# Two transformer blocks on one core: the matmuls' moving tiles are placed at the same byte modulo 512 as the weight tiles

## The chip, the cores and the metric

The kernel runs on one core of a Trainium2 chip. The metric is the device time of one execution, in microseconds (us); lower is better. Engines are called PE (TensorE, the matrix engine, with its weight loads listed apart as PEld), DVE (VectorE), ACT (ScalarE), POOL (GpSimd) and SP (SyncE, which issues most of the transfers).

## The reference

Two blocks work on a sequence of 512 positions with 1,024 channels, all in float32. The first block normalises its input, projects it, runs four heads of gated linear attention and eight heads of softmax attention with low-rank queries and keys, and multiplies the joined heads by an output matrix; a multilayer perceptron (MLP) of width 4,096 and a gated per-layer input follow. The second block has two layers: a windowed mean mixer and then a banded chunk attention of 16 heads, each followed by a gated feed-forward network (FFN) of width 2,816 with a causal convolution of three taps. Cut to what the change touches:

```
h = h + concat([o_g, o_m]) @ w_out                      # attention output parts
m = rms_norm(h); h = h + square(relu(m @ w_up)) @ w_down    # MLP, 1024 -> 4096 -> 1024
gate = sigmoid(rms_norm(h) @ w_ple_gate + b)
h = h + (p @ w_ple_proj) * gate                         # per-layer input p
x = x + pool_mixer(h) ; x = x + chunk_attention(h) @ w_o
x = x + (silu(conv3(h @ w_gate)) * (h @ w_val)) @ w_ffn_out   # FFN, 1024 -> 2816 -> 1024, twice
```

## The kernel before

**Number format.** Every large product is made of three fp32r matmuls. Each operand is split into a high part (its fp32r rounding) and a low part (the rest): weights into WH and WL, the normed input into AH and AL, the activations of the MLP and FFNs into HH and HL, the heads' outputs into OM and LM (softmax heads of the first block), OH and OL (second block) and the per-layer input into pH and pL. The helper `triple` (lines 583 to 587) issues high x high, high weight x low input, low weight x high input:

```
e.matmul(o, a, h, start=first, stop=False)      # L585: stationary WH, moving AH / HH / OM / OH / pH
e.matmul(o, a, l, start=False, stop=False)      # L586: stationary WH, moving AL / HL / LM / OL / pL
return e.matmul(o, c, h, start=False, stop=last)  # L587: stationary WL, moving AH / HH / OM / OH / pH
```

In `triple` the weights (128 columns of 4 bytes, so 512 bytes of each partition) are the stationary operand, which a weight load brings in ahead of each matmul, and the activations (512 columns, 2,048 bytes) are the moving one. `triple_t` (L591 to L593) turns the roles round: activations stationary, weights moving. It serves the value and query products and, in the mixer of the second block (`mix_rows`), HH and HL as stationary operands with 256 moving columns of the weights. A row of the profile names both operands, moving and stationary, in no fixed order of role: `bank<-HH,WH` at L585 is moving HH, stationary WH; `bank<-WH,HH` at L591 is moving WH, stationary HH.

**Order of the work.** Weights come in 136 units of up to 1 MB through two raw buffers (RAW), are rounded by ACT into one of three WH buffers (L1287) and subtracted by DVE into one of three WL buffers (L1677). PE goes through a written order (`mlp_order`, `ffn_order`, `attend_order`): for the MLP four groups of eight "up" tiles (moving AH, AL) each followed by eight "down" tiles (moving HH, HL, 8 chunks each); for each FFN three groups of 8, 8 and 6 gate and value tiles (AH, AL) and eight output tiles (HH, HL). One such run of "down" or output tiles is 8 tiles x 8 chunks x 3 = 192 matmuls, or 144 in the last group of an FFN; over the kernel that makes 8 runs of 192 and 2 of 144, 1,824 matmuls. It is called an H run below, and a run whose moving tiles are AH and AL an A run. HH and HL are written by ACT and DVE in lines 1519, 1601, 2158 and 2269 and have ten slots each.

**Memory.** `memory` places every tile by hand. An `Arena` counts upwards within a partition and rounds each size up to 32 bytes; `a.over` puts a second tile over an earlier one at a given byte. Adding up the sizes gives where each tile begins. In bytes modulo 512, called residue below: X, AH, AL, RAW, WH, WL, rb, sq, dg and t2s all begin at 256; the vectors row, r4 and m4 behind them move the shared start `base` to 64. Three layouts begin at `base`, one after the other in time:

| tiles | residue before |
|---|---|
| gq, gk, gsil, gv, low (first block's linear attention) | 64 |
| qm, km, vm, cqb | 256 |
| OM, LM (over km and qm, 3,200 bytes apart) | 256, 384, 0, 128 |
| HH, HL | 64 |
| t1s (two) | 64, 96 |
| pe_x, pH, pL, pj, zp, cvs | 128 |
| v2, qTa, kTa, OH, OL, qn | 64 |
| band (four) | 64, 64, 320, 64 |

Of the kernel before, what the change touches and what calls it, by code (L numbers as in the profile page):

```python
# [8 lines left out]
R = mybir.dt.float32r  # L9
# [6 lines left out]
P = 128  # L16
S = 512
# [7 lines left out]
MH, MN, MR, MV, MQ, MK = 8, 64, 32, 64, 96, 100  # L25
# [142 lines left out]
    pass  # L168


def memory(nc, ctx):
    k = Kit()
    a = Arena(nc, (nc.sbuf_base + 63) // 64 * 64, nc.sbuf_usable_end)
# [23 lines left out]
    k.acc = k.dg[:, :, :].rearrange("p q n -> p (q n)")  # L197
    k.ident = k.cst[:, C_ID:C_ID + P]
    k.ones = k.cst[:, C_ONE:C_ONE + P]
    base = a.at  # L200

    k.gq = a.tile("gq", [P, 2, S])
    k.gk = a.tile("gk", [P, 2, S])
# [9 lines left out]
    qm_at = a.at  # L213
    k.qm = a.tile("qm", [P, MH, 4, MK])
    km_at = a.at
    k.km = a.tile("km", [P, MH, 4, MK])
    k.OM = [a.over(f"OM{p}", [P, S], km_at + 4 * 8 * MK * p, R) for p in range(4)]
    k.msk = a.tile("msk", [P, 7, P], I32)
    k.vm = a.tile("vm", [P, 4, 512])
    cqb_at = a.at  # L220
    k.cqb = a.tile("cqb", [P, 6, S], R)
    k.cqH, k.cqL = k.cqb[:, 0:3, :], k.cqb[:, 3:6, :]
    k.tmp = a.over("tmp", [P, 6 * S], cqb_at)
# [7 lines left out]
    k.trig = k.acc.rearrange("p (i q f) -> p i q f", i=8, q=4)  # L231
    k.gb = a.over("gb", [P, 2, S], dg_at)
    k.pt1 = [a.over("pt1", [P, S], low_at), k.t2s[1]] + k.sq
    k.LM = [a.over(f"LM{p}", [P, S], qm_at + 4 * 8 * MK * p, R) for p in range(4)]
    shared = cqb_at + 4 * 2048
    k.kr = a.over("kr", [P, 4, MR], shared)
    k.krot = a.over("krot", [P, 4, MR], shared + 4 * 128)
# [14 lines left out]
    k.HH = [a.tile(f"HH{i}", [P, S], R) for i in range(NH)]  # L252
    k.HL = [a.tile(f"HL{i}", [P, S], R) for i in range(NH)]
    k.t1s = [a.tile(f"t1s{i}", [P, S + 2]) for i in range(2)]
    inner = a.at
    k.pe_x = a.tile("pe_x", [P, 2, S])
    k.pH = a.tile("pH", [P, 2, S], R)
    k.pL = a.tile("pL", [P, 2, S], R)
# [2260 lines left out]
def build(nc, W, XT, PT, PV, ROW, GW2, POS, REL, CST, MSK, BND, OUT):  # L2519
    with ExitStack() as ctx:  # L2520
        k = memory(nc, ctx)
        k.W, k.XT, k.PT, k.PV, k.ROW, k.GW2, k.POS, k.REL, k.CST, k.MSK, k.BND, k.OUT = W, XT, PT, PV, ROW, GW2, POS, REL, CST, MSK, BND, OUT
        for program in (tensor_program, vector_program, scalar_program, pool_program, sync_program):
            program(k, Dry())
        for c in (k.MM, k.WHI, k.WLO, k.ACT, k.DVE, k.POOL):
            c.n, c.known = 0, True
        block = ctx.enter_context(nc.Block())

        @block.sync
        def _(e):  # L2530
            sync_program(k, e)

        @block.tensor
        def _(e):
            tensor_program(k, e)

        @block.vector
        def _(e):
            vector_program(k, e)

        @block.scalar
        def _(e):
            scalar_program(k, e)

        @block.gpsimd
        def _(e):
            pool_program(k, e)
# [94 lines left out]
```

## Time and profile before

| | |
|---|---|
| time, median of 3 runs (lowest to highest) | 1646.34 us (1645.31 to 1647.6) |
| profiled execution, first to last instruction (its span) | 1644.3 us |
| time outside that span, against the median | 2.0 us |
| PE matmul busy | 1638.7 us, 8,084 instructions |
| PE weight loads busy | 1336.2 us, 8,084 instructions |
| DVE busy | 939.2 us |
| ACT busy | 615.9 us |
[...]

The profile gives for its own execution the span; its device time stands among no other numbers, so the 2.0 us is the difference to the median of the runs. A matmul's listed duration runs from its start to its modelled end and overlaps the next ones: 389 ns is listed for a matmul whose successor starts some 227 ns later. What a matmul costs a busy PE is therefore the distance from one start to the next, called its pitch below. It is read from a timeline: the start of one matmul less the start of an earlier one, divided by the number of matmuls between.

### The profile page before, as it was taken

How to read it: one execution, taken by the hardware profiler on the slowest of the kernel's cores; microseconds unless marked ns; L12 is line 12 of the kernel's file. 1: busy time of each engine (PE TensorE's matmuls, PEld its weight loads, DVE VectorE, ACT ScalarE, POOL GpSimd, SP SyncE). 2: the span in 40 equal slices, each digit the busy share in tenths (PEclk: the TensorE clock that was granted, in tenths of full speed). 3: DMA queues.
4: the chain of work that ended last, by engine and by line, in shares of the span. 5: the costliest groups of instructions: out<-in, count | busy, mean ns of one | idle time of the engine just before them, and what ended most of it. 6: DMA issues, size and time to landing. Idle time of an engine off the chain costs nothing.

```text
span 1644.3 us, 19097 instructions
## 1 busy us (share of the span) xinstructions
PE 1638.7 (100%) x8084; PEld 1336.2 (81%) x8084; DVE 939.2 (57%) x1385; ACT 615.9 (37%) x828; POOL 84.6 (5%) x80
## 2 busy tenths in 40 slices
PE   9999999999999999999999999999999999999999
PEld 7877878888888888888888888877777888888887
DVE  6797665444333547577466457555655576366353
ACT  5576344322332346433222223355565333122121
POOL 1300000000000000000000000311201100000000
PEclk9999999999999999999999999999999999999999
DMA  5310227454454421223322223323221223222311
GB/s 187 116 36 27 103 93 128 120 89 130 87 111 85 135 88 52 77 103 107 124 83 96 103 83 100 123 78 101 77 76 52 77 103 104 102 102 94 110 59 71
DMA packets 28054, 155.94 MB, mean 95 GB/s; under 512 B 3712, under 2 KB 5392, under 8 KB 12096
## 3 DMA queue, kind: packets, MB, share of 16 engines
q1 hardware_dynamic: 26352, 149.75, 25.6%
q0 software_dynamic: 1328, 4.86, 5.0%
q8 instruction: 64, 1.05, 0.3%
q14 instruction: 22, 0.18, 0.0%
q10 hardware_dynamic: 288, 0.10, 0.0%
HBM read 149.98 MB, written 4.72 MB: 94 GB/s over the span
## 4 chain that ended last, share of the span: by engine, by line
PE 98%; ACT 1%; DVE 1%; POOL 0%; DMA 0%; issue 0%; SPq 0%; DVEq 0%
PE bank L585 26%; PE bank L587 26%; PE bank L586 26%; PE bank L591 3%; PE bank L593 3%; PE bank L592 3%; PE bank L1216 1%; PE bank L840 1%; PE bank L1226 1%; PE bank L1242 1%; PE bank L825 1%; PE bank L865 1%; PE bank L850 1%; PE bank L769 0%; PE bank L1102 0%; PE bank L1204 0%
## 5 line engine op out<-in xcount | busy, mean ns | idle before, releaser
L585 PE MATMUL bank<-AH,WH 128*128 128x512 f32 (+1 forms) x1150 | 451.4, 393 | 0.2 <-DVE X L1707 0.2
L587 PE MATMUL bank<-AH,WL 128*128 128x512 f32 (+1 forms) x1150 | 447.8, 389 | 0.0
L586 PE MATMUL bank<-AL,WH 128*128 128x512 f32 (+1 forms) x1150 | 447.6, 389 | 0.0
L1677 DVE TENSOR_TENSOR WL<-RAW,WH 128x2048 fp32r<-128x2048 f32 (+1 forms) x133 | 298.5, 2247 | 190.7 <-ACT WH L1287 190.7
L1287 ACT ACTIVATE WH<-RAW 128x2048 fp32r<-128x2048 f32 (+1 forms) x133 | 248.3, 1871 | 260.1 <-PE bank L587 240.3
L585 PEld LDWEIGHTS bank<-AH,WH 128*128 128x128 f32 (+1 forms) x1150 | 215.5, 187 | 48.0 <-issue 2.6
L587 PEld LDWEIGHTS bank<-AH,WL 128*128 128x128 f32 (+1 forms) x1150 | 215.5, 187 | 45.8
L586 PEld LDWEIGHTS bank<-AL,WH 128*128 128x128 f32 (+1 forms) x1150 | 215.6, 187 | 45.6 <-issue 1.0
L585 PE MATMUL bank<-HH,WH 128*128 128x512 f32 x608 | 239.6, 394 | 0.0
L587 PE MATMUL bank<-HH,WL 128*128 128x512 f32 x608 | 238.4, 392 | 0.0
L586 PE MATMUL bank<-HL,WH 128*128 128x512 f32 x608 | 236.0, 388 | 0.0
L1707 DVE TENSOR_TENSOR X<-X,bank 128x512 f32<-128x512 f32 x111 | 76.0, 685 | 192.2 <-PE bank L587 192.1
L587 PEld LDWEIGHTS bank<-HH,WL 128*128 128x128 f32 x608 | 114.1, 188 | 26.8
L586 PEld LDWEIGHTS bank<-HL,WH 128*128 128x128 f32 x608 | 114.1, 188 | 25.5
L585 PEld LDWEIGHTS bank<-HH,WH 128*128 128x128 f32 x608 | 114.3, 188 | 22.8
L1596 ACT ACTIVATE t2s<-t2s,par 128x512 f32<-128x512 f32 x44 | 31.9, 724 | 186.8 <-DVE t2s L2261 186.8
L591 PE MATMUL bank<-WH,AH 128*128 128x512 f32 x224 | 90.0, 402 | 0.0
L593 PE MATMUL bank<-WH,AL 128*128 128x512 f32 x224 | 87.5, 391 | 0.0
L592 PE MATMUL bank<-WL,AH 128*128 128x512 f32 x224 | 87.3, 390 | 0.0
L1601 ACT ACTIVATE HH<-cvs 128x512 fp32r<-128x512 f32 x44 | 27.8, 632 | 126.0 <-DVE cvs L2267 126.0
L1516 ACT ACTIVATE t2s<-t1s 128x512 f32<-128x512 f32 x32 | 20.2, 632 | 97.4 <-DVE t1s L2156 97.4
L1294 ACT ACTIVATE sq<-X 128x512 f32<-128x512 f32 x49 | 30.9, 630 | 65.6 <-DVE X L1707 61.6
(306 smaller groups left out, 1732.9 us busy)
## 6 DMA issues: line engine op xcount, KB each, us to landing
RAW<-in_W SPq DMA_DIRECT2D x124, 1024.0 KB, 4.8
RAW<-in_W SPq DMA_DIRECT2D x9, 768.0 KB, 4.1
X<-in_XT SPq DMA_DIRECT2D x16, 256.0 KB, 5.5
ev_scratch<-ev POOLq DMA_DIRECT2D x16, 160.0 KB, 7.5
Gb<-ev_scratch SPq DMA_DIRECT2D x16, 128.0 KB, 2.9
Gb<-ev_scratch SPq DMA_DIRECT2D x16, 112.0 KB, 2.7
out<-X SPq DMA_DIRECT2D x7, 256.0 KB, 2.0
RAW<-in_W SPq DMA_DIRECT2D x2, 512.0 KB, 5.4
```

The lines of the kernel that those rows point to most:

```text
L585: e.matmul(o, a, h, start=first, stop=False)
L586: e.matmul(o, a, l, start=False, stop=False)
L587: return e.matmul(o, c, h, start=False, stop=last)
L591: e.matmul(o, h, a, start=first, stop=False)
L592: e.matmul(o, h, c, start=False, stop=False)
L593: return e.matmul(o, l, a, start=False, stop=last)
L1287: e.activation(k.WH[SLOT_OF[u]][:, 0:n], k.RAW[RAW_OF[u]][:, 0:n], AF.Copy).then_inc(*WHI.mark(u))
L1294: e.activation(k.acc if j == 0 else sq[(j - 1) % 2][:, :], src, AF.Square).then_inc(*ACT.mark("sqr", n, j))
L1596: e.activation(t2s[i][:, :], t2s[i][:, :], AF.Silu, bias=par[:, PC_CB + 22 * l + m:PC_CB + 22 * l + m + 1]).then_inc(*ACT.mark("silu", l, m))
L1601: e.activation(k.HH[m % NH][:, :], k.cvs[i][:, :], AF.Copy).then_inc(*ACT.mark("hh", name, m))
L1677: e.tensor_tensor(k.WL[j][:, 0:n], k.RAW[RAW_OF[u]][:, 0:n], k.WH[j][:, 0:n].bitcast(F), SUB).then_inc(*WLO.mark(u))
L1707: e.tensor_tensor(X[:, m, :], X[:, m, :], src, ADD).then_inc(*DVE.mark("x", n, m))
```

## The change

One helper is added: `in_step(at)` gives the smallest byte from `at` on whose residue modulo 512 is 256. It is applied at six places of `memory`: to `base`, to the start of cqb, to `inner` (where pe_x, pH, pL, pj, zp and cvs begin), and to each OM and LM. No instruction is added, removed or reordered.

```diff
+def in_step(at):
+
+    return (at + 255) // 512 * 512 + 256
...
-    base = a.at
+    base = a.at = in_step(a.at)
...
-    k.OM = [a.over(f"OM{p}", [P, S], km_at + 4 * 8 * MK * p, R) for p in range(4)]
+    k.OM = [a.over(f"OM{p}", [P, S], in_step(km_at + 4 * 8 * MK * p), R) for p in range(4)]
...
-    cqb_at = a.at
+    cqb_at = a.at = in_step(a.at)
...
-    k.LM = [a.over(f"LM{p}", [P, S], qm_at + 4 * 8 * MK * p, R) for p in range(4)]
+    k.LM = [a.over(f"LM{p}", [P, S], in_step(qm_at + 4 * 8 * MK * p), R) for p in range(4)]
...
-    inner = a.at
+    inner = a.at = in_step(a.at)
```

Added up again, `base` moves up by 192 bytes. HH, HL, OH, OL, v2, qTa, kTa, qn, gq, gk, gsil, gv, low, OM, LM, pe_x, pH, pL, pj, zp and cvs then begin at residue 256; cqb stays at 256; band goes to 256, 256, 0, 256; and four tiles that were at 256 leave it: qm, km, msk and vm go to 448.

## Rows read from the trace of the kernel before

**Rows 1.** The page's head and its busy times: us, share of the span, instructions.

```profile
span 1644.3 us, 19097 instructions
PE 1638.7 (100%) x8084; PEld 1336.2 (81%) x8084; DVE 939.2 (57%) x1385; ACT 615.9 (37%) x828; POOL 84.6 (5%) x80
```

**Rows 2.** The page's chain that ended last, by engine.

```profile
PE 98%; ACT 1%; DVE 1%; POOL 0%; DMA 0%; issue 0%; SPq 0%; DVEq 0%
```

**Rows 3.** The waits of PE, longest first: total us, times, longest.

```profile
PE bank L658 <- DVE rb L1729: 1.1, 1, 1.1
...
PE bank L585 <- DVE X L1707: 0.2, 1, 0.2
```

**Rows 4.** PE's groups by line and shape: busy us, mean ns, idle before.

```profile
L585 PE MATMUL bank<-AH,WH 128*128 128x512 f32 x1143 | 448.6, 392 | 0.2 <-DVE X L1707 0.2
...
L585 PE MATMUL bank<-HH,WH 128*128 128x512 f32 x608 | 239.6, 394 | 0.0
...
L1242 PE MATMUL bank<-sq,v 128*64 128x128 f32 x160 | 11.3, 279 | 0.0
...
L865 PE MATMUL bank<-sq,vm 128*64 128x128 f32 x80 | 5.6, 279 | 0.0
```

**Rows 5.** Timeline of PE at the ends of an H run and two A runs: start us, us.

```profile
820.39 0.40 PE L585 MATMUL bank<-AH,WH 128*128 128x512 f32 x1
...
907.48 0.40 PE L585 MATMUL bank<-HH,WH 128*128 128x512 f32 x1
...
951.44 0.40 PE L585 MATMUL bank<-AH,WH 128*128 128x512 f32 x1
...
995.01 0.40 PE L585 MATMUL bank<-HH,WH 128*128 128x512 f32 x1
```

**Rows 6.** Timeline of PE around the longest run with OH and OL moving.

```profile
1254.84 0.40 PE L585 MATMUL bank<-OH,WH 128*128 128x512 f32 x1
...
1278.88 0.39 PE L585 MATMUL bank<-AH,WH 128*128 128x512 f32 x1
```

**Rows 7.** Timeline of PE around the longest run with pH and pL moving.

```profile
588.78 0.40 PE L585 MATMUL bank<-pH,WH 128*128 128x512 f32 x1
...
593.90 0.40 PE L586 MATMUL bank<-pL,WH 128*128 128x512 f32 x1
```

**Rows 8.** Timeline of PE: a run with OM and LM, then one with AH and AL.

```profile
200.28 0.40 PE L586 MATMUL bank<-LM,WH 128*128 128x512 f32 x1
...
205.38 0.40 PE L587 MATMUL bank<-OM,WL 128*128 128x512 f32 x1
...
248.18 0.40 PE L586 MATMUL bank<-AL,WH 128*128 128x512 f32 x1
...
253.21 0.39 PE L587 MATMUL bank<-AH,WL 128*128 128x512 f32 x1
```

**Rows 9.** Timeline of PE in the mixer, HH and HL stationary, before and after a break.

```profile
645.20 0.28 PE L591 MATMUL bank<-WH,HH 128*128 128x256 f32 x1
...
652.15 0.28 PE L593 MATMUL bank<-WH,HL 128*128 128x256 f32 x1
...
653.85 0.28 PE L592 MATMUL bank<-WL,HH 128*128 128x256 f32 x1
...
657.71 0.28 PE L593 MATMUL bank<-WH,HL 128*128 128x256 f32 x1
```

**Rows 10.** Groups from 907 to 951 us, an H run: busy us, mean ns, idle before.

```profile
L585 PEld LDWEIGHTS bank<-HH,WH 128*128 128x128 f32 x64 | 12.0, 188 | 2.4
...
L1677 DVE TENSOR_TENSOR WL<-RAW,WH 128x2048 fp32r<-128x2048 f32 x4 | 9.2, 2292 | 5.1 <-ACT WH L1287 5.1
L1287 ACT ACTIVATE WH<-RAW 128x2048 fp32r<-128x2048 f32 x4 | 7.7, 1914 | 25.3 <-PE bank L587 25.3
```

## Prediction

> **What bounds the kernel.** I read the page's head first [rows 1]: PE is busy 1638.7 of 1644.3 us, the next engine 57%. The chain that ended last puts 98% of the span on PE [rows 2], and the waits of PE [rows 3] name five waits, the longest 1.1 us at the very start. So nothing that DVE, ACT or a transfer saves can be worth more than some 5 us, and anything that changes the pitch of a PE instruction goes straight into the time. The second reading is therefore the pitch of the same instruction with different tiles. The groups [rows 4] can't show it: 392 and 394 ns are durations that overlap. The timeline does, and it holds the change's experiment already, since AH sits at residue 256 like the weights and HH at 64, in the same line, shape, engine clock and order of three:
>
> - H run, 907.48 to 951.44 us [rows 5]: 43.96 us for 192 matmuls, a pitch of 229.0 ns.
> - The A run behind it, 951.44 to 995.01 us [rows 5]: 43.57 us for 192, 226.9 ns.
> - The A run ahead of it is twice as long, 820.39 to 907.48 us [rows 5]: 87.09 us for 384. If its first 192 take 43.57 us like the other A run's, its second 192 take 43.52, a pitch of 226.67 ns. So an A run settles at 226.67, after an entry that costs 0.05 us.
>
> None of the three holds a wait of PE, so 2.3 ns per matmul is a property of the pair of tiles and not of supply.
>
> **The change part by part.** It adds and removes no instruction; every term is a number of matmuls times a difference of pitch.
>
> 1. HH and HL, 64 to 256. All runs of the down and output projections, 1,824 matmuls (L585 to L587, 608 each [rows 4]). They get the residue pair that AH and WH have. I take AH's settled pitch: 1,824 x (228.96 - 226.67) = 4.2 us. The lower bound of this term is nothing (residue is not the cause), and below nothing is taken up as a rival.
> 2. The entries of the A runs. Eight A runs follow straight on an H run and pay the 0.05 us of entry worked out above. If all moving tiles look alike, there is no entry: 8 x 0.05 = 0.4 us. Bounds 0 and 0.4.
> 3. OH and OL, 64 to 256. Their longest run [rows 6] takes 24.04 us for 105 matmuls, 229.0 ns: the H runs' pitch, in other buffers, reached from another start. That is the strongest hint that the residue counts and not the buffer. 105 x 2.3 = 0.24 us; the other 87 or so stand in pieces of 6 or 12 between attention steps, and I leave those at nothing (bound 87 x 2.3 = 0.2 us).
> 4. pH and pL, 128 to 256. The longest run [rows 7] takes 5.12 us for 22 matmuls, 232.7 ns. A third residue, a third pitch. 24 x (232.7 - 226.7) = 0.14 us; the other 24 follow on short breaks and I leave them out (bound 0.14).
> 5. OM and LM, four residues to one. Right behind a break [rows 8] 22 matmuls take 5.10 us, 231.8 ns; with AH and AL, behind the same kind of break, 22 take 5.03 us, 228.6. Bound 96 x 3.2 = 0.3 us; half of the runs are only 12 long, where even AH doesn't settle, so I take 0.2.
> 6. HH and HL as stationary tiles in the mixer, 96 matmuls of 256 columns. Here the same tiles give two pitches [rows 9]: 6.95 us for 59 is 117.8 ns, and behind a break 3.86 us for 34 is 113.5. The trace has no matched pair of this shape. If all went to the slower, 36 x 4.3 = 0.15 us lost; to the faster, 60 x 4.3 = 0.26 gained. I take nothing. It warns that the phase in which a run starts can also set its pitch.
> 7. vm leaves residue 256 for 448, v2 comes to it from 64. Both are stationary for 128 moving columns beside sq at 256, and the groups cost the same per matmul [rows 4]: 11.3/160 and 5.6/80 us, 70 ns both, matched or not. Nothing either way, and so for the other attention operands and transposes: 320 matmuls times 1 ns would be 0.3 us.
> 8. The other engines. DVE and ACT read and write the moved tiles, but off the path. In an H run ACT's weight rounding idles 25.3 us for four instructions, waiting for PE to let a WH buffer go, and DVE's subtraction waits on ACT for 5.1 [rows 10]; a unit of 48 matmuls lasts 11.0 us against 1.9 us of ACT and 2.3 of DVE. PE 1% faster eats 0.1 us of 6.3 per unit. What is late next is still PE.
>
> Sum: 4.2 + 0.4 + 0.24 + 0.14 + 0.2 = 5.2 us. The span goes from 1644.3 to 1639.1; with the 2.0 us that lie outside it the median of 1646.34 becomes 1641.1.
>
> The rows give no mechanism, only that a weight load [rows 10] of 188 ns is under way during every matmul, from another tile of the same memory, and that the two readers' residues go with the pitch. [...]
>
> **The rivals.**
>
> - *The residue isn't the cause.* AH and HH differ also in distance from the weights (AH begins 48 KB below the first WH, HH 61 KB above it, by the tiles' sizes) and in the runs' place. If that sets the pitch, HH stays at 229.0 and the time is 1646.3, within 0.2%. For it: the mixer's two pitches with the same tiles [rows 9]. Against it: OH [rows 6] shares HH's residue and pitch from other bytes; pH [rows 7] lies beyond HH and is slower, but has another residue too, so distance alone would explain those two as well. Chance 0.14.
> - *The pitch settles half-way.* HH gets the residue but another steady pattern, as in the mixer, say 227.8: 1,824 x 1.15 = 2.1 us plus half of terms 3 to 5, 0.3; time 1643.9, 0.15% faster. For it again [rows 9]; against it that each A run settles at one pitch whatever went before. Chance 0.08.
> - *Matched is the bad case at HH's place* (slower). OM0 and LM0 are at 256 already, and their run still averages 231.8 [rows 8]; if matched tiles above the weights ran at the 231.8 of that run, the H runs would cost 1,824 x 2.8 = 5.1 us more and the time would be 1651.5. It decides from a pitch of 229.0 upwards. Against it: in that run only three matmuls in twelve have OM0 or LM0, the neighbours have other residues, and a pitch reaches across neighbours, as AH's entry shows. Chance 0.06.
> - *More than forecast*: the pieces left out in terms 3 to 7 settle too, up to 0.9 us more, and breaks get shorter; 1639.8. Chance 0.04.
>
> **How the numbers follow.** The forecast has the remaining 0.68: 1641.1 us, with a range of its own of 1639.3 to 1643.0 from the bounds of the terms (0.4 + 0.24 + 0.14 + 0.2 may be missing, 0.9 may be added) and some 1 us by which medians of the same kernel differ, as the three times shown do. A measurement tells 0.2%, 3.3 us, from no change: faster by more than that below 1643.0. Forecast and "more" give 0.72; of the half-way case a quarter falls on the faster side, of the forecast a few hundredths on the other: faster 0.71, same 0.22, slower 0.07. For 8 in 10 the range takes in the half-way case and leaves out most of "no change" and all of "slower": 1638.8 to 1645.2.
>
> **What would show it right or wrong in the changed profile.** The H run that began at 907.48 should take 43.5 us and not 44.0 for 192 matmuls (term 1), and the A run behind it 43.5 and not 43.57 (term 2); OH's run 23.8 and not 24.04; pH's 22 matmuls 4.99 and not 5.12; the run with OM 5.03 and not 5.10. The listed durations in L585 to L587 with HH should fall to AH's. DVE's and ACT's durations should stay as they are. Most of the gain is one assumption, that AH's pitch carries over to HH; if the H runs stay at 229.0, nothing is left but tenths.

## The result, and the profile after

The changed kernel takes 1640.98 us (median of 7 runs, 1640.23 to 1643.56), the kernel before beside it 1647.06 (7 runs, 1645.31 to 1647.6); the ratio is 0.9964 with a 95% interval from 0.9953 to 0.9975. The forecast was 1641.1 us and 5.2 us faster; the profiled executions are 5.6 us apart in span. The changed file's lines are five further down, so L585 is now L590.

The page's head and busy times of the changed kernel; PE's busy time fell with the span; DVE's and ACT's, 939.2 and 615.9 before, moved by 0.4 us at most:

```profile
span 1638.7 us, 19097 instructions
PE 1633.0 (100%) x8084; PEld 1335.8 (82%) x8084; DVE 938.8 (57%) x1385; ACT 616.0 (38%) x828; POOL 84.9 (5%) x80
```

PE's groups by line and shape. The mean of HH with WH, 394 ns before [rows 4], is now 389 like that of the other two H groups. AH's with WH stayed at 392:

```profile
L590 PE MATMUL bank<-AH,WH 128*128 128x512 f32 x1143 | 448.4, 392 | 0.2 <-DVE X L1712 0.2
...
L590 PE MATMUL bank<-HH,WH 128*128 128x512 f32 x608 | 236.5, 389 | 0.0
L591 PE MATMUL bank<-HL,WH 128*128 128x512 f32 x608 | 236.5, 389 | 0.0
L592 PE MATMUL bank<-HH,WL 128*128 128x512 f32 x608 | 236.5, 389 | 0.0
```

The timeline at the ends of the same runs as in [rows 5]:

```profile
817.33 0.39 PE L590 MATMUL bank<-AH,WH 128*128 128x512 f32 x1
...
904.37 0.39 PE L590 MATMUL bank<-HH,WH 128*128 128x512 f32 x1
...
947.89 0.39 PE L590 MATMUL bank<-AH,WH 128*128 128x512 f32 x1
...
991.41 0.39 PE L590 MATMUL bank<-HH,WH 128*128 128x512 f32 x1
```

The H run takes 43.52 us for its 192 matmuls (43.96 before), the A run behind it 43.52 (43.57), the long A run ahead 87.04 (87.09). 43.52 / 192 is 226.67 ns: these runs have the settled pitch from their first matmul, and the entry of the A run behind an H run is gone.

The same view around OH's long run (105 matmuls), pH's first 22, and 22 with OM right behind a break, as in [rows 6 to 8]:

```profile
1250.78 0.40 PE L590 MATMUL bank<-OH,WH 128*128 128x512 f32 x1
...
1274.62 0.39 PE L590 MATMUL bank<-AH,WH 128*128 128x512 f32 x1
...
586.34 0.39 PE L590 MATMUL bank<-pH,WH 128*128 128x512 f32 x1
...
591.32 0.39 PE L591 MATMUL bank<-pL,WH 128*128 128x512 f32 x1
...
199.93 0.40 PE L591 MATMUL bank<-LM,WH 128*128 128x512 f32 x1
...
204.96 0.40 PE L592 MATMUL bank<-OM,WL 128*128 128x512 f32 x1
```

They take 23.84, 4.98 and 5.03 us, where 24.04, 5.12 and 5.10 were before and 23.8, 4.99 and 5.03 were forecast. The third figure equals what 22 matmuls with AH take behind such a break [rows 8].

The mixer, HH and HL stationary, as in [rows 9]:

```profile
642.59 0.28 PE L596 MATMUL bank<-WH,HH 128*128 128x256 f32 x1
...
649.66 0.28 PE L598 MATMUL bank<-WH,HL 128*128 128x256 f32 x1
...
651.24 0.28 PE L597 MATMUL bank<-WL,HH 128*128 128x256 f32 x1
...
655.31 0.28 PE L598 MATMUL bank<-WH,HL 128*128 128x256 f32 x1
```

59 matmuls now take 7.07 us (6.95 before) and 34 take 4.07 (3.86), a pitch of 119.8 and 119.7 ns. Here the matched pair is slower than the pair before the change.

Where the 5.6 us came from, as the sum of start-to-next-start over all matmuls of a group, before and after, added up from every start time in the two traces:

| group | before | after | difference, us |
|---|---|---|---|
| HH, HL moving (1,824) | 417.43 | 413.21 | -4.22 |
| AH, AL moving (3,456) | 790.29 | 789.54 | -0.75 |
| OH, OL moving (192) | 46.02 | 45.82 | -0.21 |
| OM, LM moving (96) | 23.43 | 23.14 | -0.29 |
| pH, pL moving (48) | 11.63 | 11.47 | -0.16 |
| HH, HL stationary, 256 columns (96) | 11.71 | 11.93 | +0.22 |
| band moving, zp stationary (64) | 7.83 | 7.60 | -0.23 |

They add up to -5.64. Of AH's 0.75 us, 0.35 is the entries of the seven A runs that follow straight on an H run, 0.05 each, and 0.03 the like behind OH. 0.37 arose in the first A matmuls of the kernel, from 5.7 us on: the first four pitches there are 486, 427, 426 and 321 ns before the change and 434, 233, 236 and 224 after it. AH and the weights keep their bytes in both kernels, so the placing doesn't explain these 0.37 us. They go with the clock: the trace's record of the granted clock begins, at 1.00, 7.2 us into the span before the change and 6.2 us after it, behind a first 5 us in which PE was busy 3.94 us in both. No record covers the microseconds ahead of that, but 427 ns is what 512 columns take at a granted 0.50: with base alone moved (below) the record stands at 0.50 for 3.4 us from 193.1 us on, and the six matmuls that start from 193.37 us on take 2.56 us, 427 ns each. That the same level holds at the kernel's start is an estimate from this. (In the kernel before, the windows of the H and the A run of [rows 5], 907 to 951 and 951 to 995 us, both read 1.00.)

### The profile page after: what moved, and what is told of

The parts are those of the page before. It is cut to its first block, busy times and chain, and to the rows that moved or that the text cites. A ratio compares the mean times of both kernels' runs of the same rounds, so it can differ in the third digit from the quotient of the medians.

```text
span 1638.7 us, 19097 instructions
## 1 busy us (share of the span) xinstructions
PE 1633.0 (100%) x8084; PEld 1335.8 (82%) x8084; DVE 938.8 (57%) x1385; ACT 616.0 (38%) x828; POOL 84.9 (5%) x80
## 4 chain that ended last, share of the span: by engine, by line
PE 98%; ACT 1%; DVE 1%; POOL 0%; DMA 0%; issue 0%; SPq 0%; DVEq 0%
PE bank L590 26%; PE bank L592 26%; PE bank L591 26%; PE bank L596 3%; PE bank L598 3%; PE bank L597 3%; PE bank L1221 1%; PE bank L845 1%; PE bank L1231 1%; PE bank L1247 1%; PE bank L830 1%; PE bank L870 1%; PE bank L855 1%; PE bank L774 0%; PE bank L1107 0%; PE bank L1209 0%
## 5 line engine op out<-in xcount | busy, mean ns | idle before, releaser
L590 PE MATMUL bank<-AH,WH 128*128 128x512 f32 (+1 forms) x1150 | 451.2, 392 | 0.2 <-DVE X L1712 0.2
L592 PE MATMUL bank<-AH,WL 128*128 128x512 f32 (+1 forms) x1150 | 447.7, 389 | 0.0
L591 PE MATMUL bank<-AL,WH 128*128 128x512 f32 (+1 forms) x1150 | 447.6, 389 | 0.0
L590 PEld LDWEIGHTS bank<-AH,WH 128*128 128x128 f32 (+1 forms) x1150 | 215.5, 187 | 48.0 <-issue 2.4
L592 PEld LDWEIGHTS bank<-AH,WL 128*128 128x128 f32 (+1 forms) x1150 | 215.5, 187 | 45.6
L591 PEld LDWEIGHTS bank<-AL,WH 128*128 128x128 f32 (+1 forms) x1150 | 215.5, 187 | 45.4 <-issue 1.0
L590 PE MATMUL bank<-HH,WH 128*128 128x512 f32 x608 | 236.5, 389 | 0.0
L591 PE MATMUL bank<-HL,WH 128*128 128x512 f32 x608 | 236.5, 389 | 0.0
L592 PE MATMUL bank<-HH,WL 128*128 128x512 f32 x608 | 236.5, 389 | 0.0
L592 PEld LDWEIGHTS bank<-HH,WL 128*128 128x128 f32 x608 | 114.1, 188 | 23.7
L590 PEld LDWEIGHTS bank<-HH,WH 128*128 128x128 f32 x608 | 114.1, 188 | 23.7
L591 PEld LDWEIGHTS bank<-HL,WH 128*128 128x128 f32 x608 | 114.1, 188 | 23.7
```

## The experiments

Each kernel is the changed one with the edit shown. A pitch is read as above, mostly from the H run near 905 to 925 us and the A run behind it, both 192 matmuls. Where a time stands without a range it is one run, beside runs of the kernel before at 1645.4 to 1647.0; the pitches come from 192 matmuls at a time, and the H run took 43.52 us alike in the changed kernel and in the first and third below. A start is shown to 10 ns, so a pitch over 192 matmuls is good to 0.1 ns.

**The step at base alone.**

```diff
-    k.OM = [a.over(f"OM{p}", [P, S], in_step(km_at + 4 * 8 * MK * p), R) for p in range(4)]
+    k.OM = [a.over(f"OM{p}", [P, S], km_at + 64 + 256 + 4 * 8 * MK * p, R) for p in range(4)]
...
-    k.LM = [a.over(f"LM{p}", [P, S], in_step(qm_at + 4 * 8 * MK * p), R) for p in range(4)]
+    k.LM = [a.over(f"LM{p}", [P, S], qm_at + 64 + 256 + 4 * 8 * MK * p, R) for p in range(4)]
...
-    inner = a.at = in_step(a.at)
+    inner = a.at = a.at + 320
```

> Only the shared start base is moved to 256 (so HH, HL, OH, OL, v2 and the like); OM and LM keep the residues 256, 384, 0, 128, and pe_x, pH, pL, pj, zp and cvs keep 128. Theory (the pitch goes with the difference of residue between moving and stationary tile): H runs at 226.7 ns, A runs behind them without the entry of 0.05 us, OH's long run at 227.2, but pH's first 22 matmuls at 232.7 ns and the run with OM at 231.8 as before the change. Against before: 4.2 + 0.4 + 0.2 = 4.8 us faster; against the changed kernel some 0.5 us slower, less than times can tell. Rival (the gain needs all tiles): H runs above 226.7.

Median 1641.24 us (6 runs, 1640.65 to 1642.15), ratio to before 0.9967, interval 0.9955 to 0.9979. H and A runs have 226.67 ns. The timeline of pH's run, 22 matmuls:

```profile
587.54 0.40 PE L590 MATMUL bank<-pH,WH 128*128 128x512 f32 x1
...
592.66 0.40 PE L591 MATMUL bank<-pL,WH 128*128 128x512 f32 x1
```

5.12 us, 232.7 ns, as before the change. The run with OM, at 200.99 to 206.07 us here, takes 5.08 us for the 22 matmuls of [rows 8], where 5.10 was before and 5.03 with everything placed. So the terms stand by themselves: base carries nearly all the time, and pH and OM stay near their old pitches when they are left behind.

**All but the step at base.**

```diff
-    base = a.at = in_step(a.at)
+    base = a.at
```

> The changed kernel without the step at base: HH, HL, OH, OL, v2 and the others begin at 64 as before; OM, LM, pe_x, pH, pL, pj, zp, cvs are at 256. Theory: H runs at 229.0 ns again, OM's and pH's runs matched at 226.7 to 228.9; against before 0.1 (pH) + 0.2 to 0.3 (OM) = 0.3 to 0.4 us faster, 0.02%, no change that times can tell. The mixer keeps its mismatched pair and should take less than the changed kernel's 11.9 us for its 96 matmuls. Rival (the gain is not additive and one of the small steps carries it): 1641.

Median 1645.67 us (11 runs) against 1646.02 (15 runs), ratio 0.9998, interval 0.9989 to 1.0007. In its timeline the H run is back at 43.96 us, with the entry of the A run behind it:

```profile
906.37 0.40 PE L590 MATMUL bank<-HH,WH 128*128 128x512 f32 x1
...
950.34 0.40 PE L590 MATMUL bank<-AH,WH 128*128 128x512 f32 x1
...
993.91 0.40 PE L590 MATMUL bank<-HH,WH 128*128 128x512 f32 x1
```

The mixer's 96 matmuls take 11.70 us here, as before. With the run before it this splits the gain: all of it that a time can tell comes from base, and OM, pH, cqb and inner give tenths that only the pitches show.

**Everything at another residue, but all alike.**

```diff
-    return (at + 255) // 512 * 512 + 256
+    return (at + 447) // 512 * 512 + 64
...
-    x_at = a.at
+    x_at = a.at = in_step(a.at)
```

> All tiles that the change puts to 256, and X, AH, AL, RAW, WH, WL, rb, sq, dg and t2s too, begin at residue 64: every moving tile and every weight tile share a residue, but another one. Theory (only the difference counts): all long runs at 226.7 ns, time that of the changed kernel within 1 us. Rival (byte 256 itself is good and 64 bad, as HH at 64 ran at 229.0): all runs at 229 or above, some 1640.5 + 5,400 x 2.3 ns = 1653 us.

Median 1641.54 us (5 runs, 1639.98 to 1641.89), ratio 0.9963, interval 0.9949 to 0.9978; every long run has 226.67 ns. HH stands at 64 again, where it ran at 229.0 before. Byte 256 itself is nothing special: the difference counts. This and the next run end the rival by which place or distance sets the pitch.

**Five placements of AH and HH against weights that stay at 256.** `in_step` takes the residue as an argument; AH and AL, and base with HH and HL, are put where the table says, RAW and what follows it back to 256. For the first of them:

```diff
+    a.at = in_step(a.at, 320)
     k.AH = a.tile("AH", [P, 8, S], R)
...
-    raw_at = a.at
+    raw_at = a.at = in_step(a.at)
...
-    base = a.at = in_step(a.at)
+    base = a.at = in_step(a.at, 384)
```

> Weights stay at 256; AH and AL go to 320 (64 above the weights), HH, HL, OH, OL and the other tiles at base to 384 (128 above). Theory: both kinds of run get pitches of their own, different from 226.7; before the change 192 bytes below the weights gave 229.0 and 128 below gave 232.7, so I expect A runs at 228 to 236 ns and H runs at 227 to 236, the time 1641 + 3,450 x 1.5 to 9 ns + 1,824 x 0.5 to 9 ns, that is 1647 to 1689 us. Rival (the place in memory sets the pitch, not the residue): A runs stay at 226.7, H runs at 226.7 or 229.0, time 1641 to 1645.

> Weights stay at 256; AH and AL go to 64, the residue that HH had before the change (192 below the weights), HH and the other tiles at base to 448 (192 above). Theory: A runs settle at 229.0 ns, as HH did with the same residues; that alone costs 3,450 x 2.3 ns = 7.9 us against the changed kernel, 1649 us before what the H runs at their new residue add (226.7 to 236 ns, 0 to 17 us). Rival (place or distance): A runs stay at 226.7.

> Weights at 256, AH and AL at 192 (64 below), HH, HL, OH, OL and base at 0 (256 below). In the runs so far moving 64 above the weights gave 228.9 ns and 192 below gave 228.9 too, 192 above 233.35 and, with activations stationary, a moving tile 64 below its stationary one 233.4: pairs that are equal modulo 256. Theory 256 (only the difference modulo 256 counts): H runs at 226.7 ns, A runs at 233.35; time 1641 + 3,450 x 6.7 ns + 1 us = 1665 us. Theory 512 (the period is 512, as the change has it): H runs at 228 ns or more, 1668 us or more.

> Weights at 256, AH and AL 32 below, HH and base 32 above. A pitch that rises smoothly with the difference modulo 256 would give H runs some 227.8 ns (half of 64's rise) and A runs, at 224 modulo 256, between 226.7 and 233.35, some 230; time about 1641 + 3,450 x 3.3 + 1,824 x 1.1 ns = 1654 us. If only the 64-byte step counts (all within one step alike), H runs stay at 226.7 and A runs are at 233.35: 1664 us.

> Weights at 256, AH and AL 96 above, HH and base 160 above. By what lies on either side (64: 228.9, 128: 232.4 to 233.4, 192: 233.35) A runs 230.7 and H runs 233; time 1641 + 3,450 x 4.0 + 1,824 x 6.5 ns + 4 us = 1671 us. A pitch under 226.7 in either would beat the change.

The five kernels have AH and HH at (320, 384), (64, 448), (192, 0), (224, 288) and (352, 416); their times 1663.14, 1664.86, 1662.95, 1680.14 and 1682.08 us. The timelines at the start of the H run, the A run and the next H run, in that order of kernels:

```profile
915.90 0.39 PE L591 MATMUL bank<-HH,WH 128*128 128x512 f32 x1
...
960.51 0.39 PE L591 MATMUL bank<-AH,WH 128*128 128x512 f32 x1
...
1004.46 0.39 PE L591 MATMUL bank<-HH,WH 128*128 128x512 f32 x1
```

```profile
916.97 0.39 PE L591 MATMUL bank<-HH,WH 128*128 128x512 f32 x1
...
961.75 0.39 PE L591 MATMUL bank<-AH,WH 128*128 128x512 f32 x1
...
1005.71 0.39 PE L591 MATMUL bank<-HH,WH 128*128 128x512 f32 x1
```

```profile
918.01 0.39 PE L591 MATMUL bank<-HH,WH 128*128 128x512 f32 x1
...
961.55 0.39 PE L591 MATMUL bank<-AH,WH 128*128 128x512 f32 x1
...
1006.35 0.39 PE L591 MATMUL bank<-HH,WH 128*128 128x512 f32 x1
```

```profile
926.72 0.40 PE L591 MATMUL bank<-HH,WH 128*128 128x512 f32 x1
...
971.52 0.40 PE L591 MATMUL bank<-AH,WH 128*128 128x512 f32 x1
...
1016.32 0.40 PE L591 MATMUL bank<-HH,WH 128*128 128x512 f32 x1
```

```profile
927.12 0.39 PE L591 MATMUL bank<-HH,WH 128*128 128x512 f32 x1
...
972.09 0.40 PE L591 MATMUL bank<-AH,WH 128*128 128x512 f32 x1
...
1016.89 0.39 PE L591 MATMUL bank<-HH,WH 128*128 128x512 f32 x1
```

Each difference of two starts, divided by 192, ordered by moving residue less weights' residue modulo 256 (the kernels before and after included). The starts are those of the timelines here, in [rows 5] and in the changed kernel's; the time of the 192 matmuls is taken from the same trace's starts in whole ns:

| modulo 256 | modulo 512 | pitch, ns | moving tile, residues (AH, HH) of the kernel | starts, us | 192 matmuls, us |
|---|---|---|---|---|---|
| 0 | 0 | 226.67 | H at 256, changed kernel | 904.37 to 947.89 | 43.520 |
| 0 | 0 | 226.67 | A at 256, changed kernel | 947.89 to 991.41 | 43.520 |
| 0 | 256 | 226.8 | H at 0 (192, 0) | 918.01 to 961.55 | 43.540 |
| 32 | 32 | 233.3 | H at 288 (224, 288) | 926.72 to 971.52 | 44.800 |
| 64 | 64 | 228.9 | A at 320 (320, 384) | 960.51 to 1004.46 | 43.954 |
| 64 | 320 | 229.0 | H at 64, kernel before | 907.48 to 951.44 | 43.963 |
| 64 | 320 | 228.9 | A at 64 (64, 448) | 961.75 to 1005.71 | 43.951 |
| 96 | 96 | 233.4 | A at 352 (352, 416) | 972.09 to 1016.89 | 44.808 |
| 128 | 128 | 232.4 | H at 384 (320, 384) | 915.90 to 960.51 | 44.612 |
| 160 | 160 | 234.2 | H at 416 (352, 416) | 927.12 to 972.09 | 44.970 |
| 192 | 192 | 233.3 | H at 448 (64, 448) | 916.97 to 961.75 | 44.789 |
| 192 | 448 | 233.3 | A at 192 (192, 0) | 961.55 to 1006.35 | 44.800 |
| 224 | 480 | 233.3 | A at 224 (224, 288) | 971.52 to 1016.32 | 44.800 |

AH at 64 runs at 228.9 in its own place, 48 KB on the other side of the weights: the pitch of HH before belongs to the pair of residues. Three times (at 0, 64 and 192) entries equal modulo 256 and 256 apart modulo 512 agree, and H at 0 settles at 226.67 (0.1 ns more over the run is its entry behind a mismatched A run). The period is 256 bytes, not 512, and theory 512 falls. What I expected of the two kernels off the steps of 64 was wrong: a smooth rise by 26 us with AH at 224 and HH at 288, its rival by steps of 64 by 16 us, and the values between neighbours by 11 us with AH at 352 and HH at 416. There is one good residue, one a third as bad 64 above it (2.2 ns against 6.7), and all others tried lie between 232.4 and 234.2. The kernel before had its HH by chance on the second best. No residue off a multiple of 32 was measured: AH at 272 and HH at 240 were planned and have no result.

The third that the residue 64 costs is seen in a triple: with A at 320, 43.95 / 64 is 686.7 ns for its three matmuls, 6.7 more than the 680.0 of a matched triple, while with H at 288 (32) or A at 192 (192) 44.80 / 64 is 700.0 ns, 6.7 more for every one of the three.

The sign of the difference goes with the role. In the value products (`triple_t`) AH is stationary and the weights move. The first and the last matmul of a run of 96 with AH at 192, then with AH at 64:

```profile
70.10 0.39 PE L597 MATMUL bank<-WH,AH 128*128 128x512 f32 x1
...
91.86 0.39 PE L599 MATMUL bank<-WH,AL 128*128 128x512 f32 x1
```

```profile
69.25 0.39 PE L597 MATMUL bank<-WH,AH 128*128 128x512 f32 x1
...
91.41 0.40 PE L599 MATMUL bank<-WH,AL 128*128 128x512 f32 x1
```

From the first start to the last, 95 pitches, that is 229.0 ns with AH at 192 and 233.3 with AH at 64, the other way round than with AH moving (233.3 and 228.9). Moving less stationary residue, modulo 256, is 64 and 192 here, as the table has it.

**Which weight load a matmul meets.** In the changed kernel's H run the load for L591 starts at 920.01 us with the matmul of L590 and takes 0.19 us, and the matmul of L591 starts at 920.24: the next matmul's weights are loaded under each matmul. WL alone, HL alone, both, and WH alone go 128 up. `in_step(a.at, 384)` stands ahead of the tile, and what follows goes back to 256 (in the two with HL, t1s follows HL and band gives way by 128 bytes). For WL:

```diff
-    wl_at = a.at
+    wl_at = a.at = in_step(a.at, 384)
...
+    a.at = in_step(a.at)
     k.rb = a.tile("rb", [P, S])
```

> The changed kernel with WL alone moved to 384 (128 above); moving tiles, HH, AH and WH stay at 256. In each triple one of three weight loads (that of L592) is at another residue. Theory next (a start-to-start time is set by the moving tile and the weight load for the matmul after it, which runs under it) and theory own (by a matmul's moving tile and its own weights) say the same here: one of three mismatched by 128, at 232.4 to 233.4 ns, so 228.6 to 228.9 on average for A and H runs; time 1641 + 5,900 x 2.1 ns = 1653 us. Rival (only the moving tiles' residues among each other count): all at 226.7, 1641.

> The changed kernel with HL alone moved to 384; all weights and all other moving tiles stay. In an H triple L591 alone has a mismatched moving tile. Theories next and own both say 228.6 to 228.9 ns on average for H runs, A runs at 226.7; time 1641 + 1,824 x 2.1 ns = 1645 us.

> The changed kernel with WL and HL both at 384, all else at 256. H triple: L590 moves HH, L591 moves HL, L592 moves HH; the loads for them are WH, WH, WL. Theory next: under L590 the load of L591 (WH, matched), under L591 the load of L592 (WL, both at 384, matched), under L592 the load of the next L590 (WH, matched): H runs at 226.7 ns though two tiles have moved. Theory own: L591 has HL with WH and L592 HH with WL, two of three mismatched: H runs at 230.5 to 231.1. A runs in both as with WL alone moved, 228.6 to 228.9. Time: next 1641 + 4,100 x 2.1 ns = 1650 us, own 1657 us.

> The changed kernel with WH alone at 384; WL and all moving tiles at 256. Moving WL raised two of three pitches, moving HL one of three, moving both two of three in H runs. Theory either (a matmul's pitch goes from 226.7 to some 233.3 ns, once, if its moving tile differs by 128 from its own weights or from the weights loaded under it for the matmul after it) fits all three; here L590 and L591 have their own WH mismatched and L592 the next WH: three of three, A and H runs at 233.3 ns, time 1641 + 1.5 x 25.6 (what WL at 384 cost) = 1679 us. Theory next alone: L590 and L592, two of three, 231.1 ns, 1666 us. Theory own alone: L590 and L591, two of three, 231.1 ns, 1666 us. Rival (the step between one weight load and the next is what costs, which would also fit moving WL): WH to WH to WL has two steps per triple, 231.1 ns, 1666 us.

Their times are 1666.55, 1645.73, 1666.65 and 1676.17 us. The timeline of the H and the A run with WL alone moved, with HL alone moved and with WH alone moved:

```profile
918.39 0.39 PE L591 MATMUL bank<-HH,WH 128*128 128x512 f32 x1
...
962.77 0.39 PE L591 MATMUL bank<-AH,WH 128*128 128x512 f32 x1
...
1007.14 0.39 PE L591 MATMUL bank<-HH,WH 128*128 128x512 f32 x1
```

```profile
907.66 0.39 PE L591 MATMUL bank<-HH,WH 128*128 128x512 f32 x1
...
951.61 0.39 PE L591 MATMUL bank<-AH,WH 128*128 128x512 f32 x1
...
995.12 0.39 PE L591 MATMUL bank<-HH,WH 128*128 128x512 f32 x1
```

```profile
924.76 0.39 PE L590 MATMUL bank<-HH,WH 128*128 128x512 f32 x1
...
969.56 0.39 PE L590 MATMUL bank<-AH,WH 128*128 128x512 f32 x1
...
1014.36 0.39 PE L590 MATMUL bank<-HH,WH 128*128 128x512 f32 x1
```

With 226.67 matched and 233.33 mismatched, one of three mismatched gives 228.9 on average, two 231.1, three 233.3. WL moved: 231.1 in both kinds of run, two of three, where theories next and own both said one and a time 14 us shorter. HL moved: 228.9, one. Both moved: H runs 231.0, A runs 231.2, two of three. So next alone fell (it had H runs at 226.67) and own alone fell with WL alone. A third theory was made from these three: a pitch is raised, once, if the moving tile mismatches its own weights or those loaded under it for the next matmul. It was tried on WH alone, where it says three of three and each of the others, the step between weight loads too, says two. Measured: 233.3 in both runs, and a time 3 us under the 1679 expected. On average it holds in all four.

Matmul by matmul it holds in two of them. Taken from every start in the settled part of the H runs, with WL alone moved L591 has 226.7 ns (neither mismatch), L592 232.5 (only the weights loaded under it), L593 234.2 (only its own weights); with HL alone moved L592 has 234.2, L591 226.7 and L593 225.8. With both moved (L592 to L594 in that kernel) it should be L593 and L594 that rise. The triples alternate instead, one at some 224, 232 and 225 ns and the next at some 236, 234 and 235, six matmuls adding up to what the theory says for two triples. So the rule tells what a triple costs on average; which matmul pays is not settled.

## Why the prediction was right

- *What bounds the kernel*: right. PE stayed busy for the whole span, and 5.64 us of pitch made 5.6 us of span; without the 0.37 us of the kernel's start it is 5.3, beside 5.2 forecast. The medians lie 6.1 us apart (a ratio of 0.9964 is 5.9 us, its interval 4.1 to 7.7); the half microsecond above the span's difference is within that interval, and the last section shows what moves single executions by 1 us and more.
- *Term 1, AH's settled pitch carries over to HH* (4.2 us): measured 4.22. The assumption it rested on, that the residue is the cause, is shown by the kernels with all at 64 and with AH at 64.
- *Term 2, entries* (0.4): the entries are gone; the A run behind the H run fell from 43.57 to 43.52 us. The prediction counted eight such runs; there are seven, three in the MLP and two in each FFN, so 0.35 us.
- *Terms 3 to 5, OH, pH, OM* (0.24, 0.14, 0.2): measured 0.21, 0.16, 0.29. OM gained more because its last two runs of 12, left at nothing in the forecast, gained 0.05 us each.
- *Term 6, the mixer* (nothing, bounds 0.15 lost to 0.26 gained): 0.22 us lost, outside the bound. The bound took the two pitches seen for the only ones, and the matched pair had a third, 119.8 ns, above both. That is not the price of matching alone: the same 96 matmuls took 11.93 us matched (11.92 with HH at 0) and 11.93 in the kernel with HH at 416, and between 11.85 and 11.91 in every other kernel where HH or the weights stood apart, save with HH at 64 (11.71 and 11.70).
- *Term 7* left out a shape: band moving over zp gained 0.23 us and was not costed. It offsets the mixer by chance, and its cause is open (below).
- *Term 8*: right. DVE and ACT are where they were (938.8 and 616.0 us busy, 939.2 and 615.9 before).
- *The rivals*: "the residue isn't the cause" fell by the same two kernels, "matched is the bad case at HH's place" by the changed kernel's own H runs at 226.67 ns. "Half-way" had no case among 512-column runs: each pair of residues has one settled pitch, within 0.1 ns where two runs share it. The same instructions differ by up to 7.5 ns (226.67 to 234.2) by nothing but the bytes at which tiles begin.

Left open: by what means the placing of two tiles acts on the pitch. The runs show the period, the values and, on average, which loads count. They don't show why 64 is a third as bad as the rest, nor why the mixer's 256-column matmuls settle at 113.3 ns (its second run before the change) or 117.8 (its first) and with the matched pair at 120.0. The band and zp matmuls take 7.60 us in the changed kernel and with base alone moved, 7.83 before and with all but base; but the four slices of a band tile that move begin 576 bytes apart, so each of these kernels meets all four differences 0, 64, 128 and 192. The table can't explain the 0.23 us.

## What to carry to other kernels

When PE is the bound, read the pitch (226.67 ns in the changed kernel's H run), not the listed duration (389), of one instruction form with different tiles: a trace often holds the comparison already, and a property of the tile pair shows as a difference that no wait explains. For 512-column fp32r matmuls here, moving tiles and both their own and the following stationary tile should begin at the same byte modulo 256; a wrong start cost up to 3.3% of a pitch (234.2 ns against 226.67), and a change of an unrelated tile's size ahead of them can bring it in. In the tiles of the table the slices that a matmul reads lie multiples of 512 bytes apart and share their tile's residue; with another distance, as in band, each slice has a residue of its own. Other shapes must be read by themselves: at 256 columns matching gained nothing in any kernel (11.92 or 11.93 us for the mixer's 96 matmuls matched, 11.70 to 11.93 otherwise).

## What the runs showed of the hardware that was not expected

- The pitch against the residue is no slope but one good value (226.67 ns), one a third of the way up (228.9) and a plateau from 232.4 to 234.2 ns, with a period of 256 bytes in the three pairs of the table that tell it from 512.
- The settled matched pitch is 226.67 ns for 512 columns (43.520 us for 192) and 120.0 for 256 (86 of the mixer's 96 pitches in the changed kernel are 120 ns). The 256 columns between them take 106.67 ns, 0.4167 a column. An estimate from these two numbers: each pitch is that of its columns and of 32 more, 544 and 288 times 0.4167. At 32, 192 and 224 modulo 256 the pitch of 512 columns is 233.33 ns (44.800 us for 192), 16 columns' worth more again.
- In the profiled execution with base alone moved, the granted clock fell for a few microseconds, though PE was busy 40.00 of the 40 us from 150 to 190 us, ahead of them, and 10.00 of 10 from 190 to 200, in which they lie. The windows of that kernel, after them the same of the kernel before:

```profile
190.00:195.00 5.00, 5.00 (x28) 4.36 (x27) 0.71 (x2) 4.11 (x5) 1.64 (x1) 0.81 0.00 0
195.00:200.00 5.00, 5.00 (x26) 4.15 (x24) 4.87 (x6) 0.00 (x0) 0.00 (x0) 0.85 0.40 144
```

```profile
190.00:195.00 5.00, 5.00 (x42) 4.52 (x41) 0.17 (x1) 3.82 (x5) 1.64 (x1) 1.00 0.00 0
195.00:200.00 5.00, 5.00 (x32) 4.36 (x30) 4.67 (x5) 0.29 (x1) 0.00 (x0) 1.00 0.24 52
```

The column behind POOL's, PEclk, reads 0.81 and 0.85 where the other execution has 1.00; the lost share, 5 x (0.19 + 0.15), is 1.7 us, half of the 3.4 us for which the trace's record stands at 0.50, between stretches at 1.00. Seven of the fourteen traces have such a stretch, 3.4 us at 0.50 in each, which begins between 192.3 and 194.2 us; the traces before and after the change have none, and those with WL and with WH alone moved hold no record of the clock. It is the main reason why executions of one kernel lie 1.5 us apart: of 15 executions of the kernel before, beside the kernel with all but base, the nine with a mean granted clock of 1.000 took 1645.35 to 1646.10 us and the six with 0.999 took 1646.92 to 1648.13. That is more than terms 2 to 5 together, and why these had to be read as pitches.
